# One expert's weights for both halves of the middle unit, and a spare place loaded by row

## The reference

```
g_idx   = argmax over 4 groups;  e_idx = top 2 of the 8 experts inside that group
expert  = g_idx * 8 + e_idx                      # 32 experts, 512 * 2 = 1024 assignments
y       = (silu(x @ w_gate[e]) * (x @ w_up[e])) @ w_down[e]      # 1024 -> 256 -> 1024
out     = rmsnorm(x + sum over the two picks of weight * y)
```

## Time and profile before

| what | value |
|---|---|
| median of 3 runs | 1306.73 us (1304.83 to 1307.73) |
| the profiled execution | 1307.87 us, its span 1305.9 us |
| busy in the span | PE 1260.8 us (97%), DVE 610.3 us, ACT 460.5 us, POOL 532.1 us |
| DMA | 214.25 MB; from about 1080 us to 1275 us of the span 411 to 425 GB/s |
| granted TensorE clock, mean | 0.997 |

### The profile page before, as it was taken

One profiled execution on the slowest core, in us unless ns is written; L12 is line 12 of the kernel. 1 busy time (PEld: TensorE's weight loads), 2 busy tenths in 40 slices (PEclk: granted clock), 3 DMA queues, 4 the chain that ended last, 5 costly groups with the idle time before them and its releaser, 6 DMA issues.

```text
span 1305.9 us, 17416 instructions
## 1 busy us (share of the span) xinstructions
PE 1260.8 (97%) x6138; PEld 936.0 (72%) x6138; DVE 610.3 (47%) x1127; ACT 460.5 (35%) x770; POOL 532.1 (41%) x682
## 2 busy tenths in 40 slices
PE   7999999999999999999999999999999988999987
PEld 6767777787888888888888788777888863333333
DVE  4868768726542422222226765748142352222225
ACT  5657543435444323133244434154322201000002
POOL 4644323334555645545555665334653211111100
PEclk9999999999999999999999999999999989999999
DMA  7422212112334433434323343312428979999996
GB/s 224 104 65 64 66 49 65 49 50 80 109 92 118 132 87 96 141 86 140 98 87 112 92 107 84 79 41 77 123 71 321 360 289 412 424 424 425 425 425 269
DMA packets 211575, 214.25 MB, mean 164 GB/s; under 512 B 31499, under 2 KB 193021, under 8 KB 199348
## 3 DMA queue, kind: packets, MB, share of 16 engines
q1 hardware_dynamic: 202960, 203.40, 45.8%
q0 software_dynamic: 4752, 8.10, 1.7%
q10 hardware_dynamic: 3796, 1.86, 0.5%
HBM read 205.76 MB, written 16.78 MB: 170 GB/s over the span
## 4 chain that ended last, share of the span: by engine, by line
issue 38%; POOL 31%; PE 26%; DVE 3%; ACT 1%; POOLq 0%; DMA 0%; DVEq 0%; ACTq 0%
POOL wlo L629 31%; PE bank L2185 8%; PE bank L2202 4%; PE bank L1819 3%; PE bank L1821 3%; PE bank L1820 3%; PE side L1849 1%; ACT hid L1057 1%; DVE hid L1645 1%; PE bank L2224 1%; PE side L1819 1%; PE side L1821 1%; PE side L1820 1%; PE bank L2287 1%; PE side L2107 0%
## 5 line engine op out<-in xcount | busy, mean ns | idle before, releaser
L629 POOL TENSOR_TENSOR wlo<-raw,whi 128x256 fp32r<-128x256 f32 x644 | 497.6, 804 | 525.0 <-ACT whi L736 524.9
L1820 PE MATMUL bank<-actB_lo,whi 128*128 128x512 f32 x608 | 236.9, 390 | 0.0
L1819 PE MATMUL bank<-actB_hi,whi 128*128 128x512 f32 x576 | 228.0, 396 | 0.5 <-POOL wlo L629 0.5
L1821 PE MATMUL bank<-actB_hi,wlo 128*128 128x512 f32 x576 | 224.6, 390 | 0.0
L736 ACT ACTIVATE whi<-raw 128x1024 fp32r<-128x1024 f32 x161 | 169.1, 1051 | 152.1 <-PE bank L1821 124.9
L1819 PE MATMUL bank<-actA_hi,whi 128*128 128x512 f32 x400 | 157.1, 393 | 1.7 <-DVE actA_lo L1152 1.6
L1821 PE MATMUL bank<-actA_hi,wlo 128*128 128x512 f32 x400 | 155.9, 390 | 0.0
L1820 PE MATMUL bank<-actA_lo,whi 128*128 128x512 f32 x400 | 155.8, 390 | 0.0
L1820 PEld LDWEIGHTS bank<-actB_lo,whi 128*128 128x128 f32 x608 | 114.3, 188 | 24.0 <-issue 1.0
L1819 PEld LDWEIGHTS bank<-actB_hi,whi 128*128 128x128 f32 x576 | 108.2, 188 | 25.8 <-issue 2.3
L1821 PEld LDWEIGHTS bank<-actB_hi,wlo 128*128 128x128 f32 x576 | 108.2, 188 | 22.8
(11 more groups left out here) (408 smaller groups left out, 1667.3 us busy)
## 6 DMA issues: line engine op xcount, KB each, us to landing
dn<-in_w_exp_down SPq DMA_DIRECT2D x33, 1024.0 KB, 18.2
gu<-in_w_exp_gate SPq DMA_DIRECT2D x31, 1024.0 KB, 17.0
gu<-in_w_exp_up SPq DMA_DIRECT2D x31, 1024.0 KB, 19.2
raw<-in_w_in SPq DMA_DIRECT2D x57, 512.0 KB, 3.9
raw<-in_w_up SPq DMA_DIRECT2D x32, 512.0 KB, 3.9
raw<-in_w_down SPq DMA_DIRECT2D x32, 512.0 KB, 3.9
raw<-in_w_out SPq DMA_DIRECT2D x16, 512.0 KB, 3.9
raw<-in_w_in SPq DMA_DIRECT2D x16, 256.0 KB, 3.2
```

The costliest lines, as they stand in the source:

```text
L629: ins = nc.gpsimd.tensor_tensor(wlo[:, slot, at], raw[:, slot, at], whi[:, slot, at].bitcast(F32), ALU.subtract)
L1819: mm(b[:, :], w_hi, hi[:, k, :], start=first, stop=False)
L1820: mm(b[:, :], w_hi, lo[:, k, :], start=False, stop=False)
L1821: ins = mm(b[:, :], w_lo, hi[:, k, :], start=False, stop=last)
```

## The change

- **Unit 8** takes both halves from place 16's weights: rows 0 to 63 and 64 to 127 of one expert, the first with overflow (or expert 31 if there is none). If that expert is one of 16 to 31 it is left out of the later order, and the other fifteen take places 17, 19, 20, ... 32, by expert numbers that SP reads from `over_n`. Place 18 (SPARE) is then empty. It is loaded by POOL with three indirect DMAs whose rows 1 to 127 lie out of bounds in that case, so that one row each is moved; in the other case it is expert 31 in full.
- The lists of rows for units 8 to 16 (`placed`, the second table, `list_overflow`) depend on that, so the first table covers 8 columns instead of 16, and `count_overflow` and `place_overflow` on DVE get further steps.
- **ye is gone.** `y_of` writes into `xe`; the scatter reads it there. The gather into the same buffer now waits until the scatter has landed, and comes one unit later in POOL's order.
- PE turns rows two units ahead; the first quarter of the next unit's gates stands in two parts around `turn_hidden` for units 1 to 8 (AHEAD_E). Gates and ups are separate instructions (256 columns) in all units, and wait for separate semaphores.
- SP: unit 4 too is loaded in quarters (PIECED_E); units 12 to 16 load both gates before both ups.
- The "values" table comes before `turn_rows_of(0)`, with other counts of `keep_busy`; the second table's work moves from unit 0 to unit 1.

```diff
+LATE = PAIRS
+EVENS, ODDS = PAIRS + 8, PAIRS // 2 + 1
+SPARE = 2 * EXTRA_AT + 2
+def halves_of(q):
+    return places_of(q) * (2 if q == EXTRA_AT else 1)
+PIECED_E = range(GU_BUFS // 2, GU_BUFS // 2 + 2)
+AHEAD_E = range(1, EXTRA_AT + 1)
 ...
 # SP
+                    at = 1 if n == 2 * EXTRA_AT else 1 + OVER + late_at(n)
+                    late[n] = sp.value_load(over_n[0:1, at:at + 1], min_val=0, max_val=NE - 1)
 ...
+            for q in range(PIECED_E.start, EXTRA_AT + 1):
                 for n in places_of(q):
+                    if n >= D_BUFS:
+                        sp.wait_ge(S("down_done"), unit_of(n - D_BUFS) + 1)
+                        down(n)
+                if q in PIECED_E:
+                    gate_up_in_quarters(q)
+                    continue
 ...
+                if q >= EXTRA_AT + 4:
+                    for h in range(2):
+                        for n in ours:
+                            load_gate_up(n % GU_BUFS, expert_of(n), landed_of(n), (h,))
 # POOL
+            def spare_expert():
+                spare_bound = pool.to_reg(NE * P - 1)
+                pool.wait_ge(S("gate_up_done"), unit_of(SPARE - GU_BUFS) + 1)
+                pool.wait_ge(S("down_done"), unit_of(SPARE - D_BUFS) + 1)
+                for to, name in ((gu[SPARE % GU_BUFS][:, 0, :, :], "w_exp_gate_2"), ...):
+                    pool.indirect_dma_start(to..., None, A[name][0]...,
+                                            bass.IndirectOffsetOnAxis(ap=spare_rows[:, 0:1], axis=0),
+                                            bounds_check=spare_bound, oob_is_err=False).then_inc(S("spare_in"), 16)
 ...
             for q in range(LAST_E):
-                pool.wait_ge(S("y_made"), q + 1)
-                scatter(q % 2, ...)
-                n = q + X_BUFS
-                if n < UNITS_E:
-                    gather(n % X_BUFS, ...)
+                n = q - 1 + X_BUFS
+                if X_BUFS <= n < UNITS_E:
+                    pool.wait_ge(S(f"scattered{(q - 1) % 2}"), 16 * ((q - 1) // 2 + 1))
+                    gather(n % X_BUFS, tabi[:, 1, n:n + 1], S(f"gathered{n % X_BUFS}"))
+                if q == EXTRA_AT - 1:
+                    spare_expert()
+                pool.wait_ge(S("y_made"), q + 1)
+                scatter(q % X_BUFS, tabi[:, 0, q:q + 1], S(f"scattered{q % 2}"))
 # DVE
+            def y_of(q):
+                dve.wait_ge(S("down_done"), q + 1)
+                for n in range(2):
+                    x = xe[:, q % X_BUFS, n * L:(n + 1) * L]
+                    ins = v.scalar_tensor_tensor(x, bank[2 + n][:, :], slotv[:, 1, q:q + 1], x, ALU.mult, ALU.add)
+                ins.then_inc(S("y_made"), 1)
 ...
             rows_turned(0, 1)
             list_values()
-            place_overflow()
+            count_overflow()
             for q in range(LAST_E):
                 hidden(...)
-                rows_turned((q + 1) % 2, q + 2)
                 if q == 0:
+                    rows_turned(1, 2)
+                    y_of(0)
+                if q + 2 < UNITS_E:
+                    rows_turned(q % 2, q + 3)
+                if q == 0:
+                    place_overflow()
+                    continue
+                if q == 1:
                     list_overflow()
                 y_of(q)
 # PE
+            keep_busy(bank[0], 4)
+            turn_rows_of(0)
             for q in range(LAST_E):
                 gate_up_of(q)
-                turn_rows_of(q + 1)
                 if q == 0:
+                    turn_rows_of(1)
+                elif q + 2 < UNITS_E:
+                    turn_rows_of(q + 2)
+                if q == 1:
                     pe.wait_ge(S("over_placed"), 1)
                     ... the second table ...
+                first_gates_of(q + 1, 0)
                 turn_hidden(q % 2, q + 1)
+                first_gates_of(q + 1, 1)
                 down_of(q)
+                if q == 0:
+                    turn_rows_of(2)
```

More of the change, by code:

```diff
@@ L506, in _, with landed_of @@
                                 for n in ("w_exp_gate_2", "w_exp_up_2", "w_exp_down_2"))
+            def landed_of(n):
+                return [S(f"{w}_in{unit_of(n) % TURNS}") for w in ("gates", "ups")]
             def load_gate_up(n, e, loaded, halves=(0, 1)):
@@ L1085, in _ @@
                 act.wait_ge(S("final_sum"), n + 1)
[L1086 removed]
+                chain(a(xe[:, 1 + n, :], y2[:, n, 0, :], ACT.Square, accum_out=gw[:, 12, n:n + 1]))
                 guess(gw[:, 12, n:n + 1], 10 + n, gw[:, 13, n:n + 1], D, gw[:, 14, n:n + 1], False)
@@ L1679, in place_overflow @@
                 chain(v.scalar_tensor_tensor(pos[:, :], pos_q[:, :], -float(ROWS), pos[:, :], ALU.mult, ALU.add))
+            def place_overflow():
+                before, column_of = prod[:, 0, 3 * NE:4 * NE], prod[:, 1, NE:2 * NE]
+                first_at, at_odd = (flat[:, 2 * NT * n:2 * NT * (n + 1)] for n in range(2))
                 chain(v.tensor_tensor(at_row[:, :, :], rows64.unsqueeze(1).broadcast_to([P, 2 * NT, ROWS]),
                                       every(pos[:, :], ROWS), ALU.is_equal))
-                mine = placed[:, :, 0, :]
@@ L1698, in list_overflow @@
-                slot, back = (prod[LOW_ROWS, 0, w * OVER:(w + 1) * OVER] for w in range(2))
-                chain(v.tensor_scalar(slot, table[:, 0:OVER], float(SKIP), None, ALU.add))
-                chain(v.tensor_scalar(back, slot, float(L), -float(L), ALU.is_ge, ALU.mult))
-                chain(v.tensor_tensor(tabi[LOW_ROWS, 1, EXTRA], slot, back, ALU.add))
-                chain(v.tensor_copy(tabi[LOW_ROWS, 0, EXTRA], slot))
-                chain(v.tensor_copy(slotv[LOW_ROWS, :, EXTRA], table[:, OVER:].rearrange("p (n c) -> p n c", n=2)), S("over_listed"))
@@ L1705, in y_of @@
-            def y_of(q):
-                y_out(q % 2, q % X_BUFS, slotv[:, 1, column(q):column(q) + 1], q + 1,
-                      S(f"scattered{q % 2}") if q >= 2 else None, 16 * (q // 2))
+                for rows, of, to in ((slice(0, P), slice(0, ODDS), slice(EXTRA_AT, EXTRA_AT + ODDS)),
+                                     (LOW_ROWS, slice(ODDS, EVENS), EXTRA)):
+                    table = late_table(rows, of)
+                    slot, back = (prod[rows, 0, w * EVENS:w * EVENS + of.stop - of.start] for w in range(2))
+                    chain(v.tensor_scalar(slot, table[:, 0, :], float(SKIP), None, ALU.add))
+                    chain(v.tensor_scalar(back, slot, float(L), -float(L), ALU.is_ge, ALU.mult))
+                    chain(v.tensor_tensor(tabi[rows, 1, to], slot, back, ALU.add))
+                    chain(v.tensor_copy(tabi[rows, 0, to], slot))
+                    chain(v.tensor_copy(slotv[rows, :, to], table[:, 1:3, :]), S("over_listed") if rows == LOW_ROWS else None)
@@ new lines, in gate_up_of @@
+            def gate_up_of(q):
+                for i, (g, ks) in enumerate(QUARTERS_E):
+                    if i == 0 and q in AHEAD_E:
+                        continue
+                    ins = gate_up_part(q, g, ks)
+                    if i == len(QUARTERS_E) - 1:
+                        ins.then_inc(S("gate_up_done"), 1)
+                    elif q <= PIECED_E.stop - 1 - PIECED_E.start:
+                        ins.then_inc(S("quarter_used"), 1)
+                    elif q == LAST_E and i == 1:
+                        ins.then_inc(S("last_gates_done"), 1)
@@ L2236, in _, with first_gates_of @@
+            def first_gates_of(q, part):
+                if q in AHEAD_E:
+                    ins = gate_up_part(q, 0, slice(2 * part, 2 * part + 2))
+                    if part and q <= PIECED_E.stop - 1 - PIECED_E.start:
+                        ins.then_inc(S("quarter_used"), 1)
             over = None
-            turn_rows_of(0)
             pe.wait_ge(S("values_placed"), 1)
             table_of(bank[2], "values").then_inc(S("values_full"), 1)
+            keep_busy(bank[0], 4)
+            turn_rows_of(0)
```

281 lines of the change are left out of this document (143 added, 138 removed).

## The result

| | before | after |
|---|---|---|
| median (6 runs each, side by side) | 1306.51 us | 1317.18 us (1314.84 to 1318.16) |
| ratio, 95% interval | | 1.0077 [1.0067, 1.0088] |
| span of the profiled execution | 1305.9 us | 1315.5 us |
| granted clock, mean | 0.997 | 0.99 |
| bytes moved | 214.25 MB | 211.38 MB |

The change makes the kernel 10.7 us slower by the medians, 9.6 us by the spans of the profiles. The prediction (1300.5, range to 1306.3) was wrong, in its sign too.

The account below looks back on a forecast made before the run. PE's own work bounds the kernel, with full DMA engines close behind. +1.0 and +2.8 (start, clock), -8.0 (units 2 to 7), +0.1 (unit 8), -2.1 (load waits) sum to -6.2: 1300.5 us, range 1296.6 to 1306.3.

Parts of the forecast that it names:

- The start: Up to unit 2: later start of unit 2, +1.0 us, and a fall of PE's clock, +2.8 us.
- The standstill: PE in unit 0 waits 3.5 us for xeT of unit 1, queued on DVE behind the longer count.
- The load that goes: One of 33 places dropped, 7.4 us less DMA time; unit 8's second half costs PE only +0.1 us.
- The rival on rows out of bounds: Place 18's skipped rows cost as if moved, or the expert isn't 16 or later; 1304.5 us, chance 8%.
- The 7.4 us: DMA time of one dropped place: 3 x 1.049 MB at 424 GB/s.
- The chain: Units 2 to 8: each gather waits for its scatter's landing; no stall expected; as a rival, mostly 1305 us, chance 24%.
- the threshold: PE's row turning doesn't stall if scatter plus gather take under 14.85 us.
- S + G: Scatter time plus following gather time on POOL's queue, taken as 7.8 and 7.0 us.
- The formula: From unit q-1's down matmuls' end, rows for unit q+3 are ready after S + G + 2.04 us; PE comes at 16.9.
- The sign case: Units 3 to 13 late from S + G of about 16.8: +5 us or more, 1311 us; chance 8%.
- Units 10 to 15: PE's two waits for loads, before units 14 and 15, both go: -2.1 us.
- the tail: Behind 1282.90 us, unit 16's down matmuls onward: DMAs and order unchanged, so no change in time.

Follow-up runs that it names:

- all mended, without the three DMAs: Against the changed kernel: y in its own tile from unit 2, count split, second table in unit 2, place 18's three DMAs left out; 1301.94 us, ratio 0.9966.
- place 18 in full: Changed kernel with own y tile, split count, later second table; SP loads place 18 fully (expert 31 again) instead of the three POOL DMAs; 1308.81 us, ratio 1.0019.
- DMAs early: Against all mended: place 18's gate and up DMAs leave in unit 6, the down one in unit 7, with their own semaphore; 1304.22 us, ratio 0.998.
- gap filled: Against DMAs early: 4 multiplications of ones added on PE in unit 15 between its gates and turn_hidden; 1302.87 us, ratio 0.9975.
- all mended: Against the changed kernel: own y tile from unit 2, count split, second table in unit 2, place 18's DMAs spread over units 5, 6, 7; 1307.96 us, ratio 1.0014.

## Why the prediction was wrong

- **The start: right.** +3.3 for +3.8. The standstill was 3.32 for 3.5, the clock fell and cost 3.0 for 2.8, and splitting the count leaves 1.17 us of the wait and no fall. The second table's wait was 0.75 for 1.2.
- **The load that goes: wrong, the largest miss.** The step "The three indirect DMAs that stand for place 18 move one row each; issue on POOL 1.0 us each, in time POOL has" priced them on the issuing engine alone. Each held the queue for about 3 us, and the scatter, the next gather and unit 9 stood behind them: +7.1 for +0.1, and leaving the DMAs out gives exactly this 7.1 back (11.0 by the medians, of which 4.4 in the profiles lies elsewhere). The rival on rows out of bounds came near, but priced their bytes (7.4 us of DMA time that isn't gained), not the queue. What was said against it, that skipped rows carry no bytes, was true (0.02 MB for all three) and didn't help: each still had 144 packets. The 7.4 us themselves were well worked out (6.9 once PE could use them). The Trainium skill (DMA: Bandwidth & Descriptors, Anatomy of one DMA — SWDGE (gpsimd) path) has 2.0 us plus bytes over 436 GB/s; these three carried one row each and landed after 9.6 to 13.0 us, and after 7.4 and 6.8 with 16 listed rows, so no sum by bytes gives them.
- **The chain: the threshold right, the value chosen wrong.** S + G was 7.95 + 9.16 = 17.1 in unit 3 and 16.2 to 17.1 after, above the 14.85 that I worked out; I took 7.8 + 7.0. The formula holds: in unit 3 PE reaches the turning 17.2 us after unit 1's down matmuls end (16.9 predicted), the rows are there after 17.1 + 2.04, and the wait by that is 1.9 for the measured 1.96. With the queue to itself the gather did get quicker, by its median over the span from 9.6 to 7.7, but on the chain it took 7.7 to 9.4 and the scatter 7.7 to 8.5; the 6.1 of the earlier trace rows was taken before the DMA engines were full. Of the 8.1 us missing in units 2 to 7, 4.6 are the waits (1.96, 0.98, 1.66), 1.6 are six units of 12.09 for 11.83 (two quarters and `turn_hidden` take 1.01 + 0.37 + 0.92 by their starts, for 0.87 + 0.30 + 0.87), and the rest, 1.9, stands mostly beside the lower clock behind the wait in unit 3.
- **The sign case** named this stretch, S + G from 16.8, and +5. The sign turned through another place.
- **Units 10 to 15:** both load waits went (-2.1). Not seen in the prediction: with rows turned two units ahead, unit 15 has none to turn beside its wait for the hidden rows; that wait grew to 1.49 and the clock fell behind it, +1.7.
- **Right besides:** 2 x 256 columns cost what 512 do, unit 8's second half costs PE nothing, SP's loads didn't limit, the tail is the same.

With both queue effects and the count mended (the DMAs of the gates and ups a unit earlier) the kernel comes to 1304.22, with the gap of unit 15 filled too to 1302.87, against 1306.59: 2.4 and 3.7 us of the predicted 6.2. The profile of the first of these has unit 16 6.9 us earlier than before (1267.03), but its median gains 2.4; that profiled execution was 2.6 us below its own median, and what differs from run to run isn't settled.

## What to carry to other kernels

Price an indirect DMA in three places: its issue, its landing, and how long it holds the one queue of its engine; the last went with the rows listed (128 or 16), not the rows moved, and everything behind it in that queue is late. Put such DMAs where what is queued behind them has slack, a whole unit ahead of the reader. Reusing a tile in place puts the write's landing and the next read's landing in series; work out the sum against PE's period with the longest landings of the loaded stage, not with the one taken in a quiet one. Before putting a difference of two medians down to an edit, see in which stretch the profiles differ: here 4.4 of 11.5 us stood where the edit can't act or were lower clock. When one of two near limits is relieved, look at what the other work was hiding, and count a standstill of PE twice where the clock falls behind it.

## What the runs showed of the hardware

- An indirect DMA from POOL with 128 listed rows, 127 of them out of bounds, held its queue for 2.7 to 3.3 us; with 16 listed rows 0.6 to 1.2 us. POOL's own issue was 0.99 and 0.88 us. The packets were 144 and 32 for each.
- PE's clock didn't answer to the length of a wait alone. In unit 3, waits for the gather of 1.96 (the changed kernel), 2.00 (all mended, without the three DMAs) and 2.14 us (place 18 in full) were followed by the lower clock; waits of 1.97 (the DMAs left out), 1.99 (the count split), 2.04, 2.09 and 2.12 (DMAs early, gap filled, all mended) weren't; unit 15's wait of 1.49 or 1.50 was followed by a fall in eight kernels and by none in three. The changed kernel's stretches of one us beside the wait in unit 3, columns as in the earlier trace rows:

```profile
1111.00:1112.00 1.00, 0.58 (x4) 0.58 (x5) 0.00 (x0) 0.00 (x0) 0.00 (x0) 0.92 1.03 426
1112.00:1113.00 1.00, 1.00 (x6) 0.73 (x4) 0.68 (x1) 0.00 (x0) 0.00 (x0) 0.50 1.07 438
```

The level is 0.50 of 2.4 GHz, that is 1.2 GHz, for some three us. What decides between the two outcomes at the same wait stays open.
